# A mixture-of-experts layer that reads its routed rows back in two parts

## The reference, cut to what matters

```python
idx = top 6 of 64 experts for each token;  w = their scores, normalized, times 2.5
y = sum over the six of  w * (silu(x @ w_gate[e]) * (x @ w_up[e])) @ w_down[e]     # hidden width 256
y = y + shared_expert(x)
out = layer_norm(2 ** 0.25 * x + y, ln2_g, ln2_b)
```

## Time and profile before

| | before |
|---|---|
| runs shown, median (lowest to highest) | 1812.22 us (1811.25 to 1813.48) |
| profiled execution, its time | 1810.13 us |
| its span | 1808.3 us |
| mean granted TensorE clock | 0.991 of full speed |
| busy: TensorE, VectorE, ScalarE, GpSimd | 1729.3, 645.2, 304.9, 136.8 us |
| moved by DMA | 330.78 MB, mean 183 GB/s |

### The profile page before, as it was taken

One profiled execution on the slowest core, in us unless ns is written; L12 is line 12 of the kernel. 1 busy time (PEld: TensorE's weight loads), 2 busy tenths in 40 slices (PEclk: granted clock), 3 DMA queues, 4 the chain that ended last, 5 costly groups with the idle time before them and its releaser, 6 DMA issues.

```text
span 1808.3 us, 20139 instructions
## 1 busy us (share of the span) xinstructions
PE 1729.3 (96%) x7961; PEld 888.7 (49%) x7961; DVE 645.2 (36%) x966; ACT 304.9 (17%) x448; POOL 136.8 (8%) x141
## 2 busy tenths in 40 slices
PE   6999999999999999999999999999999999898967
PEld 3444456666666656556555454533333333333323
DVE  5011018888888884300111687500000000000008
ACT  1111112111111101112000121022222122121212
POOL 0000000000000000000000111511111111111100
PEclk9999999999999999999999999999999999999989
DMA  6115101101101001111116203789999999999848
GB/s 226 46 47 163 47 24 35 36 24 35 35 23 35 23 0 35 46 50 49 41 52 220 106 24 148 304 359 425 422 424 423 422 423 422 420 407 413 341 187 357
DMA packets 104981, 330.78 MB, mean 183 GB/s; under 512 B 8496, under 2 KB 64848, under 8 KB 86736
## 3 DMA queue, kind: packets, MB, share of 16 engines
q1 hardware_dynamic: 91520, 292.05, 41.0%
q0 software_dynamic: 13392, 37.77, 5.3%
HBM read 307.24 MB, written 33.55 MB: 188 GB/s over the span
## 4 chain that ended last, share of the span: by engine, by line
PE 82%; DMA 8%; DVE 7%; issue 1%; ACT 1%; SPq 0%; POOL 0%; DVEq 0%; POOLq 0%; ACTq 0%
PE pA L1038 15%; PE pg L671 11%; PE pg L698 10%; PE pg L821 9%; PE pB L1064 7%; PE pB L852 5%; DMA rA<-w_e_gate_up 4%; PE pB L901 2%; PE pA L901 2%; PE pA L844 2%; PE pg L711 2%; PE pB L754 2%; DMA rA<-y_dram 2%; PE pg L1025 2%; DMA rEF<-w_e_gate_up 2%; PE pA L791 1%
## 5 line engine op out<-in xcount | busy, mean ns | idle before, releaser
L698 PE MATMUL pg<-rA,hw 128*128 128x384 f32 x768 | 259.6, 487 | 0.7 <-ACT aTr L1174 0.7
L1038 PE MATMUL pA<-rCD,aTr 128*32 128x512 f32 (+2 forms) x720 | 210.0, 602 | 11.6 <-DMA rA<-w_e_gate_up 11.1
L1760 DVE TENSOR_TENSOR rows<-rows,pA 128x256 f32<-128x256 f32 x45 | 18.9, 421 | 530.9 <-ACT rows L1282 530.9
L671 PE MATMUL pg<-rEF,rA 128*128 128x512 f32 x448 | 195.1, 598 | 3.1 <-ACT rCD L1153 3.1
L698 PEld LDWEIGHTS pg<-rA,hw 128*128 128x128 f32 x768 | 140.7, 190 | 84.0 <-ACT aTr L1174 0.9
L821 PE MATMUL pg<-rA,hw 128*128 128x384 f32 x512 | 165.3, 486 | 0.0
L671 PEld LDWEIGHTS pg<-rEF,rA 128*128 128x128 f32 x448 | 85.7, 192 | 109.8 <-issue 109.8
L821 PEld LDWEIGHTS pg<-rA,hw 128*128 128x128 f32 x512 | 97.3, 190 | 67.5
L1038 PE MATMUL pA<-rA,aTr 128*32 128x512 f32 (+2 forms) x384 | 125.1, 609 | 0.0
L1038 PE MATMUL pA<-rB,aTr 128*32 128x512 f32 (+1 forms) x368 | 107.7, 599 | 5.1 <-DMA rEF<-w_e_gate_up 4.4
L1038 PE MATMUL pA<-ew,aTr 128*32 128x512 f32 (+1 forms) x352 | 107.7, 605 | 0.0
(11 more groups left out here) (324 smaller groups left out, 2331.6 us busy)
## 6 DMA issues: line engine op xcount, KB each, us to landing
rCD<-w_e_gate_up SPq DMA_DIRECT2D x21, 2048.0 KB
rA<-w_e_gate_up SPq DMA_DIRECT2D x11, 2048.0 KB, 30.9
rB<-w_e_gate_up SPq DMA_DIRECT2D x11, 2048.0 KB, 27.8
ew<-w_e_gate_up SPq DMA_DIRECT2D x11, 2048.0 KB, 32.1
rEF<-w_e_gate_up SPq DMA_DIRECT2D x11, 2048.0 KB, 32.0
rCD<-w_e_down SPq DMA_DIRECT2D x21, 1024.0 KB, 31.7
hw<-w_in SPq DMA_DIRECT2D x40, 512.0 KB, 4.1
rA<-w_e_down SPq DMA_DIRECT2D x11, 1024.0 KB, 33.5
```

The source lines that it names most:

```text
L671: last = mm(big_bank(fill), x1T[:, c, i * P:(i + 1) * P], strip[n % 2][:, c, :], start=(c == 0), stop=(c == KC - 1))
L698: last = mm(pg[:, n * 512:n * 512 + HALF], hw3[m][:, c, :], x1T[:, c, n * HALF:(n + 1) * HALF], start=(c == 0), stop=(c == KC - 1))
L1038: last = mm(gu[n][o:o + w, :], xT[n][:, c, o:o + w], at(gate_up_home(j % NB)[0], gate_up_home(j % NB)[1] + c * F, [[2 * D, 2], [1, F]]), s ...
```

## The change

The turn order is changed: rank 0 gets two units, so the rooms fill 45 rounds exactly, and ranks 4, 3, 2 and 1 come last, each alone in a round. The first 41 rounds (EARLY) scatter to `y_dram` as before. The last four and the rest blocks scatter with an add into two zeroed arrays `late0_dram` and `late1_dram` that have one row per token (and 128 rows for empty places), by the parity of the round. As a token may miss any of its six rows in `y_dram`, that too is zeroed in the places that are read.

A tile's six early rows are read during the last rounds: tiles 0 to 2 behind `y_filled` 41, 42 and 43 and the scatters of 41 rounds, ahead of the rest block's weights on SP; tiles 3 and 4 behind them; tile 5, whose buffer the rest block uses, in the tail. VectorE adds the rows of tiles 0 to 3 one by one: tile 0's before `hidden(44)`, tiles 1 and 2 before the rest loop, tile 3 after it. TensorE adds those of tiles 4 and 5. In the tail only two late rows per token are read.

The zeros are written by SP from a cleared third of `hw`: two tiles behind each of strips 2, 3 and 4, and both late arrays at the end. The column weight that needs this third and the first scatter wait for them.

```diff
@@ rooms, ranks_in_turn
+LATE = 4
-    return [1] + [4] * 10 + [3] * 32 + [2] * 21
+    return [2] + [4] * 10 + [3] * 32 + [2] * 21
     first, small = small[:4], small[4:]
+    large, alone = large[:-LATE], large[-LATE:]
-    return first + [r for _, r in mixed] + [0]
+    return first + [r for _, r in mixed] + [0] + alone
+EARLY = NR - LATE
+ZEROED = 16 * (NT + 2)
@@ sync: strips
+                if n >= 2:
+                    for i in (2 * n - 4, 2 * n - 3):
+                        sp.wait_ge(zero_ready, 1)
+                        sp.dma_start(yb[i * P:(i + 1) * P, 0:TOPK, :],
+                                     at(hw, 2 * D, [[0, TOPK], [1, D]])).then_inc(y_zeroed, 16)
+            for y in late_dram:
+                sp.dma_start(y.rearrange("(t p) n -> p t n", p=P),
+                             at(hw, 2 * D, [[0, NT + 1], [1, D]])).then_inc(y_zeroed, 16)
             sp.wait_ge(x1_ready, NT)
...
             for m, c0 in enumerate((C_Q, C_FF, C_FB)):
+                if m == 2:
+                    sp.wait_ge(y_zeroed, ZEROED)
                 sp.dma_start(hw3[m], w_in[:, :, c0:c0 + DK]).then_inc(s_hw[m], 16)
@@ sync: behind the list of weights
+            def load_early_rows(i):
+                sp.dma_start(land[i], yb[i * P:(i + 1) * P, 0:TOPK, :]).then_inc(s_yb[i], 16)
+            sp.wait_ge(y_stored[0], 16 * ((EARLY + 1) // 2))
+            sp.wait_ge(y_stored[1], 16 * (EARLY // 2))
+            for i in range(3):
+                sp.wait_ge(y_filled, EARLY + i)
+                load_early_rows(i)
             more = E % NB
             sp.wait_ge(resti_ready, 1)
...
-            sp.wait_ge(y_filled, NR)
+            for i in range(3, NT - 1):
+                sp.wait_ge(y_filled, EARLY + i)
+                load_early_rows(i)
+            sp.dma_start(ln2_g, d["ln2_g"].to_broadcast([P, D])).then_inc(s_ln2, 16)
+            sp.dma_start(ln2_b, d["ln2_b"].to_broadcast([P, D])).then_inc(s_ln2, 16)
+            def load_late_rows(i):
+                sp.wait_ge(yb_used, TOPK * (i % 4 + 1))
+                for n in range(2):
+                    sp.dma_start(late[i][:, n, :], late_dram[n][i * P:(i + 1) * P, :]).then_inc(s_late[i], 16)
             sp.wait_ge(y_stored[1 - ODD], 16 * ((NR + 1 - (1 - ODD)) // 2))
...
-            for i in range(NT):
-                if i == NB - 1:
-                    sp.wait_ge(sum_filled, 1)
-                    sp.wait_ge(yb_used, 2)
-                n = i % (NB - 1)
-                for m in range(2):
-                    three = slice(3 * m, 3 * m + 3)
-                    sp.dma_start(land[n][:, three, :], yb[i * P:(i + 1) * P, three, :]).then_inc(s_yb[n][m], 16)
+            for i in range(3):
+                load_late_rows(i)
+            load_early_rows(NT - 1)
+            for i in range(3, NT):
+                load_late_rows(i)
@@ tensor: the tail
+            pe.wait_ge(y_ready, nrest + NR)
+            early_rows_summed(4)
+            late_rows_added(4)
+            early_rows_summed(5)
+            late_rows_added(5)
@@ vector: tables, rounds, tail
-            v.tensor_scalar(tblti[:, 0:NCOL], tbldi[:, 0:NCOL], 3, None, ALU.logical_shift_right).then_inc(tb_ready, 1)
+            v.tensor_scalar(tblti[:, 0:NCOL], tbldi[:, 0:NCOL], 3, None, ALU.logical_shift_right).then_inc(tok_ready, 1)
+            ve.wait_ge(tok_ready, 1)
+            link(v.tensor_copy(tbld[:, EARLY:NCOL], tblti[:, EARLY:NCOL]))
+            link(v.tensor_scalar(tbld[:, EARLY:NCOL], tbld[:, EARLY:NCOL], float(-T), con[:, K_IOTAP:K_IOTAP + 1],
+                                 ALU.add, ALU.min))
+            v.tensor_scalar(tbldi[:, EARLY:NCOL], tbld[:, EARLY:NCOL], float(T), None, ALU.add).then_inc(tb_ready, 1)
+            def early_rows_added(i):
+                ve.wait_ge(s_yb[i], 16)
+                for k in range(TOPK):
+                    v.tensor_tensor(acc[:, i, :], acc[:, i, :], land[i][:, k, :], ALU.add).then_inc(yb_used, 1)
+                    ve.wait_ge(yb_used, TOPK * i + k + 1)
             for t in range(NR):
                 hidden(t)
+                if t == NR - 2:
+                    early_rows_added(0)
+            early_rows_added(1)
+            early_rows_added(2)
             with ve.Fori(0, nrest) as r:
...
             def summed(i):
+                if i < 4:
+                    ve.wait_ge(s_late[i], 32)
+                    v.tensor_tensor(acc[:, i, :], acc[:, i, :], late[i][:, 0, :], ALU.add).then_inc(late_used, 1)
+                    ve.wait_ge(late_used, i + 1)
+                else:
+                    ve.wait_ge(sum_filled, i - 3)
                 v.scalar_tensor_tensor(out=acc[:, i, :], in0=acc[:, i, :], scalar=1.0,
+                                       in1=late[i][:, 1, :] if i < 4 else sums[i][:, :],
...
+            early_rows_added(3)
             summed(0)
@@ gpsimd
+            g.memset(zeros, 0.0).then_inc(zero_ready, 1)
...
                 po.wait_ge(y_ready, t + 1)
+                if t == 0:
+                    po.wait_ge(y_zeroed, ZEROED)
+                if t < EARLY:
                     g.indirect_dma_start(d["y_dram"], bass.IndirectOffsetOnAxis(tbldi[:, t:t + 1], 0), yrow[t % 2], None,
                                          bounds_check=T * KSTRIDE - 1, oob_is_err=False).then_inc(y_stored[t % 2], 16)
+                else:
+                    g.indirect_dma_start(late_dram[t % 2], bass.IndirectOffsetOnAxis(tbldi[:, t:t + 1], 0), yrow[t % 2], None,
+                                         bounds_check=T + P - 1, compute_op=ALU.add).then_inc(y_stored[t % 2], 16)
```

More of the change, by code:

```diff
@@ L70 @@
 ODD = NR % 2
+EARLY = NR - LATE
+assert STARTS[E - LATE] == EARLY * UNITS and EARLY % 2 == ODD
 def most_rest_blocks():
@@ L324, in gate_up_home @@
             return ((rA, 0), (rCD, 0), (rB, 0), (ew, 0), (rEF, EW), (rCD, EW))[n]
[L326 to L330, removed]
+        land_at = [(E - LATE - 1 + i) % NB for i in range(NT)]
+        assert len(set(land_at)) == NT and land_at[NT - 1] == E % NB
+        land = [slabs(weights[n], TOPK) for n in land_at]
+        late = [land[i % 4][:, 1 + 2 * (i // 4):3 + 2 * (i // 4), :] for i in range(NT)]
+        normal = [land[i % 4][:, 5 * (i // 4), :] for i in range(NT)]
+        squares = land[2][:, 3, :]
+        ln2_g, ln2_b = hw[:, 0:D], aTr[:, 0:D]
+        zeros = hw[:, 2 * D:3 * D]
         xg = [hw[:, n * D:(n + 1) * D] for n in range(2)]
@@ L351, in build @@
         pairY = [pB, pX]
+        late_dram = [d["late0_dram"], d["late1_dram"]]
+        sums = {4: pB, 5: pX}
         sh_out = [pX[:, 0:512], pB[:, 0:512]]
@@ L471, in build @@
         y_stored = [sem(f"y_scattered{n}") for n in range(2)]
-        s_yb = [[sem(f"routed_rows_loaded{n}_{m}") for m in range(2)] for n in range(NB - 1)]
+        zero_ready = sem("zeros_ready")
+        y_zeroed = sem("routed_rows_zeroed")
+        s_yb = [sem(f"early_rows_loaded{i}") for i in range(NT)]
+        s_late = [sem(f"late_rows_loaded{i}") for i in range(NT)]
         mean_ready = sem("row_means_ready")
-        yb_used = sem("last_routed_rows_added")
+        yb_used = sem("early_rows_added")
+        late_used = sem("late_rows_added")
         sum_filled = sem("routed_rows_summed")
-        sum_taken = sem("routed_sums_taken")
+        sum_taken = sem("row_sums_ready")
         out_ready = sem("out_ready")
@@ L1109, in _, with early_rows_summed, late_rows_added @@
                 last.then_inc(xt_filled, 1)
[L1111 to L1120, removed]
-                    for m in range(2):
-                        last = mm(pairY[i % 2][:, m * 512:(m + 1) * 512], ident,
-                                  land[n][:, k, m * 512:(m + 1) * 512], start=(k == 0), stop=(k == TOPK - 3))
-                last.then_inc(sum_filled, 1)
+            def early_rows_summed(i):
+                pe.wait_ge(s_yb[i], 16)
+                for k in range(TOPK):
+                    for m in range(2):
+                        mm(sums[i][:, m * 512:(m + 1) * 512], ident, land[i][:, k, m * 512:(m + 1) * 512],
+                           start=(k == 0), stop=False)
+            def late_rows_added(i):
+                pe.wait_ge(s_late[i], 32)
+                for k in range(2):
+                    for m in range(2):
+                        last = mm(sums[i][:, m * 512:(m + 1) * 512], ident, late[i][:, k, m * 512:(m + 1) * 512],
+                                  start=False, stop=(k == 1))
+                last.then_inc(sum_filled, 1)
+            pe.wait_ge(y_ready, nrest + NR)
[3 more added lines that the diff above has]
+            late_rows_added(5)
         @block.scalar
@@ L1773, in summed @@
             def summed(i):
[L1774 to L1780, removed]
+                if i < 4:
[4 more added lines that the diff above has]
+                    ve.wait_ge(sum_filled, i - 3)
+                v.scalar_tensor_tensor(out=acc[:, i, :], in0=acc[:, i, :], scalar=1.0,
+                                       in1=late[i][:, 1, :] if i < 4 else sums[i][:, :],
```

(2 more changed lines are left out.)

17 lines of the change are left out of this document (8 added, 9 removed).

## The result

| | before | after |
|---|---|---|
| runs, median (lowest to highest) | 1812.22 us (1811.25 to 1813.48) | 1830.07 us (1827.60 to 1833.07) |
| ratio to before, with its 95% interval | | 1.0099, 1.0080 to 1.0118 |
| profiled execution; its span | 1810.13; 1808.3 us | 1831.82; 1829.9 us |
| mean granted TensorE clock | 0.991 | 0.980 |
| moved by DMA; written to HBM | 330.78; 33.55 MB | 363.70; 59.77 MB |

The account below looks back on a forecast made before the run. The routed stage was taken as near a balance of TensorE and saturated DMA, followed by a 60.6 us tail. Terms 9.8 + 6.5 + 1.7 - 19.0 + 0.7 + 0 = -0.3 gave 1812 us, no change; range 1800 to 1824.

Parts of the forecast that it names:

- B: Rest block's weights, queued on SP behind early tiles: a wait of 4.7 us and 1.8 slow start, +6.5 (0 to 9).
- 12.7 MB at 424 is 30.1 us: From 1711.2, queue carries early rows, gate-up weight and three scatters; with 2.4 us latency the weight lands at 1743.7.
- D: Tail from last scatter's landing to the end: 41.6 us instead of 60.6, -19.0 (-20 to -9), VectorE bounding.
- twelve and four more: TensorE's matmuls for tile 5 in the tail, after tile 4's four, 0.45 us each: VectorE waits 1.3 us.
- C: Last scatter, now accumulating and partly in traffic, lands 5 us after issue instead of 3.3: +1.7 us (0 to 7.4).
- A: New order of turns in routed rounds: expert 58 comes a round earlier, round 44 starts at 1723.4, +9.8 us (0 to 13).
- E: Three more VectorE operations before tb_ready, 0.21 us each, delay gather and first round: +0.7 us.
- F: Zeroing writes of 26.2 MB during the first strips: 0 us with 2.6 of cover, up to 5 if writes are slower.
- slower rival: Five accumulating scatters on one queue, each twice a plain one; the last gates late reads: 1818 or 1827 us, chance 0.25.
- from a landing of 8.6 us: Slower rival's deciding sign: the last scatter lands at least 8.6 us after its issue (5 + 3.6).
- second price, 1827: Slower rival's time if the last scatter lands 20 us after its issue; its first price was 1818 at about 11.
- estimate of 1.2 us: Accumulate's read of its destination, half a megabyte more at 424 GB/s on the last scatter: 1.2 us, giving 1813.

## Why the prediction was wrong

**B, the first half of the miss.** The step "12.7 MB at 424 is 30.1 us" failed twice. First the bytes: 15.2 MB passed between 1711 and the weight's landing. SP's queue carried 1.5 MB more than the early tiles and the gate-up weight (13.09 less 11.54). Its bytes from 1711 to the end (DMA view, 1711 to 1830) say whose they are:

```profile
q1 hardware_dynamic: 4063, 32.71, 66.8%
```

The transfers issued on it in that time add up to 32.5 MB, so only 0.2 MB was a rest of earlier ones. The other 1.3 belong to transfers issued behind the weight (the down weight, tiles 3 and 4), which the prediction counted only after it. GpSimd's queue carried 0.9 more. Second the rate: 362 GB/s instead of 424, where scatters that add hold the engines twice as long for a MB (5.0 against 2.4 us); without adding it was 408. The wait was 13.5 us, forecast 4.7; of these 8.8 the run without adding takes away 3.2 (10.3 are left) and so leaves 5.6 to the bytes; 2.4 MB at 424 GB/s would be an estimated 5.7. The slow start was 2.7 instead of 1.8 us, at a granted clock of 0.73 from 1753 to 1763.

**D, the other half.** The step "twelve and four more", at 0.45 each, was mis-sized. The earlier trace rows showed x16 for what the code calls eight times: a call is two instructions here. Tile 5's twelve calls took 10.30 us, not 5.4; tile 4's four took 6.37 from idle, not 3.3; tile 5's last four 3.45, not 1.8. Together 20.1 instead of 10.5, and VectorE's waits were 12.6 instead of 1.3. All else in D held within about 1 us: first addition 4.8 us after the landing (4.9), late tiles 5.6 apart (5.8), tile 4's late rows there after 23.4 (22.2).

**C.** The landing was 6.44 us, against 5, within its ends of 3.3 and 10.7. The same scatter without adding took 3.67, so the adding is 2.8 us of it. The scatter began 10.4 us later than forecast (1771.05, not 1760.6), with little traffic left beside it: 112 GB/s from 1770 to 1780.

**A.** Round 44 at 1722.60 against 1723.4 looks exact, but 3.1 us of it are the late start; the term itself was +6.0, and +6.1 with the turns alone. So that 1723 came true is in part luck. The long transfer that was forecast ahead of round 39 came earlier, and it was a down weight (1611.42 to 1646.38); the count of five rounds after expert 58's was right.

**E and F.** F was right. Of the 3.1 us before round 0, the tables are about 0.8: the median of the five runs without them on the path has the first product at 1176.1, of the five with them (the changed kernel is one) at 1176.9, but runs of one kind differ by as much. Some 1.4 are slow matmuls behind an unchanged gap (below). Of the remaining 0.9, some 0.7 are there at 1040 (line 941 at 1040.67, line 901 before at 1039.97); this is not explained, and neither the zeroing nor the turns alone bring it.

**The rivals.** The slower rival put the whole loss on the adding scatter and decided "from a landing of 8.6 us". The last one landed after 6.4, those of the rounds after 14.2 (median; without adding 12.3; the earlier trace rows 10.7), so it did not decide there. Its second price, 1827, comes near the result in part by luck: with the adding taken away 5.0 of the 18 us come back (medians), and the rest has other reasons. What was missing from the list is the case that happened: rest weights that wait much longer, with a tail that is bound by TensorE. The Trainium skill (DMA: Bandwidth & Descriptors, "Rules for kernel authors") says that an accumulate reads its destination and writes it later. The sign agrees with these runs, but the estimate of 1.2 us from the bytes was short of the 2.8 us measured.

**The causes taken together.** Before, the 60 us tail moved 426 GB/s (1770 to 1780) while ahead of it, in 1720 to 1730, only 57 GB/s were moved. The change does fill that room; what it meets there are three transfers that the chain hangs on (the rest weights, tile 0 ahead of a product, the last scatter), and a fourth on GpSimd's queue (the gather for a next rest block). The runs moved the wait between these, and no order tried freed all of them. How much of the last scatter's 15 to 21 us is the queue ahead of it and how much the tiles beside it was only tested in part: taking tile 4 away gave 6 us, taking the adding away 6.6.

## What to carry to other kernels

An idle stretch of DMA ahead of a tail is free only if nothing on the critical chain lands in it; before moving bytes there, list every transfer that is awaited in the stretch, and count what is issued after it as traffic beside it, too (here 1.3 MB). Price a scatter that adds at twice a plain one's engine time, as measured here, unless a trace says otherwise. When a count of calls in the code is multiplied by a duration from a row, divide the row by its own x-count first.

## What was not expected of the hardware

A scatter that adds also held GpSimd longer: 1.55 to 1.63 us in the rounds and 1.92 for the last, against 0.97 to 1.01 and 1.33 for the same scatters without adding.

The same shared-expert matmuls, behind the same gap of 2.8 us, ran at another granted clock. TensorE's timeline of the changed kernel:

```profile
1130.56 0.69 PE L971 MATMUL pX<-con,rows 128*128 128x128 f32 x2 [2.78 <-DVE rows L1618]
1131.04 8.44 PE L961 MATMUL pB<-rCD,rEF 128*128 128x512 f32 x16
```

and the window of that stretch (columns as above):

```profile
1131.00:1140.00 9.00, 9.00 (x23) 4.29 (x22) 1.93 (x7) 0.87 (x3) 0.00 (x0) 0.84 1.02 428
```

A granted clock of 0.84 is a part of the stretch at the lower level (1.2 of 2.4 GHz). The kernel before took 7.03 us for the same sixteen, at 1130.12 and at 1.00, after a gap that ended 0.7 us earlier in the span. The changed kernel and all nine runs built on it show 0.76 to 0.84 from 1131 to 1138; the three others (before, turns alone, zeroing alone) show 1.00. In the ten the gap ends at 1130.3 or later, in the three by 1130.1. What decides it was not tried.
